# Down projections of a two-layer fp32 trunk: 16 of 22 row groups by Strassen's scheme, with DVE and ACT splitting the weights

## The chip, the core and the metric

The kernel runs on one core of one Trainium2 chip. The metric is the device time of one execution in microseconds, the median of several runs. All data are fp32. TensorE (PE) multiplies; VectorE (DVE), ScalarE (ACT) and GpSimd (POOL) work on data in SBUF, DVE and ACT also in PSUM; SyncE (SP) issues most DMAs.

## What is computed

Two residual layers on 512 tokens of 1024 channels. Each has a token mixer (forgetting attention, then an RG-LRU block), a layer norm, a gated ConvFFN, a second layer norm and a gated embedding. The change is in the ConvFFN's down projection, with D_FF = 2816:

```python
def conv_ffn(x, w_up, conv_w, conv_b, w_down):
    hdn = x @ w_up
    hdn = causal_dwconv(hdn, conv_w, conv_b)
    val, gate = jnp.split(hdn, [D_FF], axis=-1)
    return (jax.nn.gelu(gate) * val) @ w_down
...
        x = layer_norm(ALPHA * x + ff, ln2_g[i], ln2_b[i])
```

## The kernel before

**Precision.** Each fp32 operand is split into a high part (rounded to fp32r) and a low part (the difference). A product is three matmuls: high x high, high x low, low x high. `three` (L436) and `token_three` (L453) issue them, at L439 to L441 and L458 to L460.

**Weights.** They stream from HBM in units of 512 KB (128 partitions x 1024 elements) into four stages `stage`. SP loads a unit when POOL has split the one before it in that stage (`unit_split`, waits and loads up to L363). POOL then writes `w_hi` (L419) and, in four pieces, `w_lo` (L425) of one of four slots, as soon as PE has used the unit four places earlier (`unit_used`). `plan` (L120) lists the phases and slots in the order qkv, out0, up0, down0, ple0, gate0, rgx, rgg, out1, up1, down1, ple1, gate1, and every wait is a count in that order: `Phase.done(i, r)` is the count of a unit, `stage_free` and `slot_free` the counts at which its stage and slot are free. Each engine runs its own queue in program order.

**Up phase.** 11 iterations of four units (`up_phase`): a value and a gate tile for each of two halves, in PSUM banks 0 to 3, 24 matmuls a unit. For each half ACT applies the last tap of the convolution (L1436), DVE the two others (L1139, L1142), ACT the gelu (L1439), DVE the product (L1149); then ACT copies it to `h_hi` (L1442) and DVE subtracts to `h_lo` (L1154). DVE's and ACT's loops (both named `conv_ffn`, L1129 and L1425) are hardware loops over the 11 iterations. So `h` lies as 22 row groups of 128 channels by 512 tokens.

**Down phase** (`down_phase`, L794). The stationary operand is a 128 x 128 tile of `h` (channels x tokens), the moving one 512 output channels of a weight row. A unit holds two row groups for one half of the 1024 output channels, so there are 22 units a layer. For half 0 all four token tiles go through the 22 row groups side by side in four banks (4 x 22 x 3 matmuls). Half 1 does so for 16 row groups and finishes the last 6 token tile by token tile, with the transposes of the first normed tiles between (`turn_tile`).

**After it.** DVE adds `ALPHA * x` to each bank (`summed`, L969), normalises and writes `x` (L977, L982); `norm_low` (L987) writes `x_lo`. The embedding's input is loaded by ACT into the place of `x_hi` once the up phase is over (L1449).

What a wait on the weights looks like on PE, and on SP:

```python
            def unit_ready(ph, i, r):
                pe.wait_ge(unit_split, ph.done(i, r))
...
                        sp.wait_ge(unit_split, ph.stage_free(i, r))
```

## Time and profile before

| | |
|---|---|
| median of 3 runs | 1255.85 us (1255.59 to 1255.9) |
| profiled execution: span (the only time shown for it) | 1254.0 us |
| PE busy | 1246.9 us, 99% |
| PE weight loads | 1016.7 us, 81% |
| DVE busy | 551.0 us, 44% |
| ACT busy | 410.2 us, 33% |
| POOL busy | 861.5 us, 69% |
| DMA | 120.61 MB, 96 GB/s over the span |

The span runs from the first to the last instruction, so what lies around it is not in it. Busy times are of the profiled execution. Matmuls are pipelined: each is listed with its full length although the next starts before it ends, so what PE really spends on one is the distance of two starts. "x<-y" names what an instruction writes and reads; the bracket at the end of a timeline line is how long its engine had been idle and what ended that.

### The profile page before, as it was taken

What the parts mean: (1) busy time and instruction counts of PE and PEld (TensorE: products, weight loads), DVE (VectorE), ACT (ScalarE), POOL (GpSimd) and SP (SyncE); (2) the same over time, 40 slices, a digit from 0 to 9 for tenths busy, and PEclk for the clock granted to TensorE, in tenths of its full rate; (3) what the DMA queues carried; (4) which work ended last, traced back from release to release, by engine and by line L of the source; (5) the groups of instructions that cost most, each with busy time, mean ns of one, the idle gap of its engine ahead of it and who ended that gap; (6) DMA issues with size and microseconds to landing.
All of it is one profiled execution on the core that took longest, in us unless ns stands there. A gap on an engine that the chain in (4) does not pass through costs nothing.

```text
span 1254.0 us, 17715 instructions
## 1 busy us (share of the span) xinstructions
PE 1246.9 (99%) x5829; PEld 1016.7 (81%) x5829; DVE 551.0 (44%) x880; ACT 410.2 (33%) x684; POOL 861.5 (69%) x1154
## 2 busy tenths in 40 slices
PE   9999999999999999999999999999999999999998
PEld 6887777788888888888888778888888888888887
DVE  6556556564443444410444374364444443201352
ACT  4445444123434333100144484114343434100041
POOL 7555467629888777776577557929887787767573
PEclk9999999999999999999999999999999999999999
DMA  5221233303322233433143222312323224333221
GB/s 197 69 67 67 67 117 101 101 17 107 110 87 99 100 128 90 118 101 101 67 168 101 85 67 84 132 37 101 102 99 100 100 90 128 118 101 98 70 93 59
DMA packets 57292, 120.61 MB, mean 96 GB/s; under 512 B 3760, under 2 KB 36080, under 8 KB 56736
## 3 DMA queue, kind: packets, MB, share of 16 engines
q1 hardware_dynamic: 56192, 117.45, 28.8%
q10 hardware_dynamic: 1056, 2.58, 0.6%
q8 instruction: 26, 0.43, 0.1%
q14 instruction: 18, 0.15, 0.0%
HBM read 117.83 MB, written 2.20 MB: 96 GB/s over the span
## 4 chain that ended last, share of the span: by engine, by line
PE 97%; ACT 1%; DVE 1%; DMA 1%; issue 0%; DVEq 0%; ACTq 0%; SPq 0%
PE bank L439 19%; PE bank L440 19%; PE bank L441 19%; PE bank L458 9%; PE bank L459 8%; PE bank L460 8%; PE bank L735 2%; PE bank L740 2%; PE bank L733 2%; PE bank L554 1%; PE bank L541 1%; PE bank L467 1%; PE bank L525 1%; PE bank L523 1%; PE bank L909 1%; PE bank L910 1%
## 5 line engine op out<-in xcount | busy, mean ns | idle before, releaser
L425 POOL TENSOR_TENSOR w_lo<-stage,w_hi 128x256 fp32r<-128x256 f32 x800 | 593.8, 773 | 29.5 <-issue 1.5
L419 POOL TENSOR_SCALAR w_hi<-stage 128x1024 fp32r<-128x1024 f32 x200 | 213.8, 1069 | 172.8 <-PE bank L460 74.5
L439 PE MATMUL bank<-x_hi,w_hi 128*128 128x512 f32 (+1 forms) x712 | 275.7, 387 | 0.0
L441 PE MATMUL bank<-x_hi,w_lo 128*128 128x512 f32 (+1 forms) x712 | 275.3, 387 | 0.0
L440 PE MATMUL bank<-x_lo,w_hi 128*128 128x512 f32 (+1 forms) x712 | 275.3, 387 | 0.0
L439 PEld LDWEIGHTS bank<-x_hi,w_hi 128*128 128x128 f32 x712 | 133.7, 188 | 27.3
L441 PEld LDWEIGHTS bank<-x_hi,w_lo 128*128 128x128 f32 x712 | 133.7, 188 | 27.2
L440 PEld LDWEIGHTS bank<-x_lo,w_hi 128*128 128x128 f32 x712 | 133.7, 188 | 26.8
L1139 DVE SCALAR_TENSOR_TENSOR tmp<-bank,cols,tmp 128x511 f32<-128x511 f32 x88 | 66.0, 750 | 201.0 <-ACT tmp L1436 190.0
L458 PE MATMUL bank<-w_hi,h_hi 128*128 128x512 f32 x352 | 137.3, 390 | 0.0
L459 PE MATMUL bank<-w_lo,h_hi 128*128 128x512 f32 x352 | 137.0, 389 | 0.0
L460 PE MATMUL bank<-w_hi,h_lo 128*128 128x512 f32 x352 | 137.0, 389 | 0.0
L417 POOL TENSOR_TENSOR waiter<-waiter 128x1 f32<-128x1 f32 x101 | 21.2, 210 | 167.7 <-PE bank L441 112.2
L439 PE MATMUL bank<-in_hi,w_hi 128*128 128x512 f32 x312 | 130.0, 417 | 0.0
L441 PE MATMUL bank<-in_hi,w_lo 128*128 128x512 f32 x312 | 122.1, 391 | 0.0
L440 PE MATMUL bank<-in_lo,w_hi 128*128 128x512 f32 x312 | 122.0, 391 | 0.0
L969 DVE SCALAR_TENSOR_TENSOR bank<-x,bank 128x512 f32<-128x512 f32 x32 | 22.2, 693 | 191.3 <-PE bank L460 190.4
L1436 ACT ACTIVATE tmp<-bank,cols 128x512 f32<-128x512 f32 x88 | 63.8, 775 | 62.1 <-PE bank L441 60.8
L1294 ACT ACTIVATE norm_stat<-norm_stat 128x1 f32<-128x1 f32 x16 | 3.3, 206 | 227.6 <-DVE norm_stat L998 227.6
L460 PEld LDWEIGHTS bank<-w_hi,h_lo 128*128 128x128 f32 x352 | 66.1, 188 | 13.9
L458 PEld LDWEIGHTS bank<-w_hi,h_hi 128*128 128x128 f32 x352 | 66.1, 188 | 13.5
L459 PEld LDWEIGHTS bank<-w_lo,h_hi 128*128 128x128 f32 x352 | 66.1, 188 | 13.5
(180 smaller groups left out, 1804.6 us busy)
## 6 DMA issues: line engine op xcount, KB each, us to landing
stage<-w_square SPq DMA_DIRECT2D x163, 512.0 KB, 3.3
stage<-w_down SPq DMA_DIRECT2D x44, 512.0 KB, 3.7
rows<-norm_rows SPq DMA_DIRECT2D x4, 1024.0 KB, 5.7
outT<-x SPq DMA_DIRECT2D x7, 256.0 KB, 2.0
x<-xT SPq DMA_DIRECT2D x3, 512.0 KB, 6.8
p_in<-pT ACTq DMA_DIRECT2D x2, 512.0 KB, 3.2
w_ai<-w_lru SPq DMA_DIRECT2D x1, 1024.0 KB, 8.9
stage<-w_square ACTq DMA_DIRECT2D x1, 512.0 KB, 7.1
```

The source lines that it names most:

```text
L419: whole = pool.tensor_scalar(high[:, s, :], stage[:, s, :], 1.0, 0.0, ALU.mult, ALU.add)
L425: piece = pool.tensor_tensor(low[:, s, to], stage[:, s, to], high[:, s, to].bitcast(F32), ALU.subtract)
L439: pe.matmul(out, w_hi[:, s, c:c + P], m_hi, start=first, stop=False)
L440: pe.matmul(out, w_hi[:, s, c:c + P], m_lo, start=False, stop=False)
L441: return pe.matmul(out, w_lo[:, s, c:c + P], m_hi, start=False, stop=last)
L458: pe.matmul(four(out), m_hi, wide_hi, start=first, stop=False)
L459: pe.matmul(four(out), m_hi, wide_lo, start=False, stop=False)
L460: return pe.matmul(four(out), m_lo, wide_hi, start=False, stop=last)
L733: pe.matmul(at_banks[r][:, at], w_hi[:, s, c:c + P], x_hi[:, k, at], start=(k == 0), stop=False, skip_group_check=early > 0)
L735: pe.matmul(at_banks[r][:, at], w_lo[:, s, c:c + P], x_hi[:, k, at], start=False, stop=False, skip_group_check=early > 0)
L1139: dve.scalar_tensor_tensor(t[:, 1:SEQ], banks[r][:, 0:SEQ - 1], cols[:, bass.ds(c + 1, 1)], t[:, 1:SEQ], ALU.mult, ALU.add)
L1436: act.activation(tmp[:, r, :], banks[r][:], ACT.Identity, bias=cols[:, bass.ds(c + 3, 1)], scale=cols[:, bass.ds(c + 2, 1)]).then_inc(conv ...
```

## The change

The last 6 row groups of each layer's down projection stay as they were. The first 16 are taken in 8 pairs (`PRE`), one for each of the first 8 iterations of the up phase. For a pair, tokens, channels and output channels are each cut in two, and the 8 block products become 7 (Winograd's form), on sums of blocks.

- **Sums of h.** `gated_part` writes the product of the first 8 iterations unsplit into `folded`, and DVE's `fold_sides` forms four sums of 256 tokens. `h_hi` and `h_lo` remain for the last 6 row groups only.
- **Two loops on PE** (`fold_phase`). The first runs 3 products for each pair (18 matmuls, banks 6 and 7, 4 and 5, 0 and 1), the second 4 products (24 matmuls, adding in banks 4 to 7 and 0, 1, and in banks 2 and 3). Between the loops, and after the second, DVE adds banks into `x` (`block_fold`), and PE waits for it (`bank_folded`).
- **Units.** There are 32 fold units a layer instead of 16, each of the 16 loaded twice, in six stages: two more, `stage_far`, lie in the place of `x_hi` and `x_lo`, which the up phase reads to its end. So do two of the three pairs `side_hi`, `side_lo`.
- **Sums of weights.** In the first loop DVE adds the two blocks of the even unit (`first_sums`, 512 elements a partition). In the second POOL issues a DMA that adds one block of 256 KB from HBM onto the odd unit (`near_sum`), and DVE makes two sums from that (`second_sums`).
- **Splits.** ACT copies to the high part (`side_top`, `unit_top`), DVE subtracts to the low part (`side_low`, `unit_low`), for the sums of h as for the weights. POOL splits only the last six units of a down phase, after all of the fold units.
- **Order.** DVE's and ACT's up loops are written out instead of looped. The last half of the last iteration (convolution, gelu, product, split) is moved behind the end of the up phase, in between the steps 0 to 5 of the first loop.
- **Layer norm.** For the second norm `x` is already scaled and the bank is added plainly.

The diff, cut to its core:

```diff
+def fold_stage(r):
+    return [3, 0, 1, 2][r] if r < 4 else [3, 0, 4, 5, 1, 2][(r - 4) % FOLD_STAGES]
...
+            def down_loads(layer, ph):
+                for r in range(FOLD_UNITS):
+                    last = fold_before(r)
+                    if r < SLOTS:
+                        sp.wait_ge(unit_split, ph.stage_free(0, r))
+                    elif last is not None:
+                        sp.wait_ge(unit_split, ph.done(0, last))
+                    else:
+                        sp.wait_ge(unit_used, phases[f"up{layer}"].done(2 * FT // 4 - 1, 3))
+                    half = 1 - r % 2 if r < FOLD else r % 2
+                    sp.dma_start(staged(r).rearrange("p (a n) -> p a n", a=4),
+                                 down_unit(layer, half, r % FOLD // 2)).then_inc(fold_loaded[fold_stage(r)], 16)
...
+            def near_sum(layer, i):
+                r = FOLD + 2 * i + 1
+                pool.wait_ge(fold_loaded[fold_stage(r)], fold_fills(layer, r))
+                pool.dma_start(pair_of(staged(r))[:, :, 0, :], down_unit(layer, 0, i)[:, :, 0:P],
+                               accum_op=ALU.add).then_inc(near_summed[fold_stage(r)], 16)
...
+            def fold_product(layer, step, r, part, pos, bank, first, last):
...
+                for tau in range(2):
+                    to = slice(tau * P, (tau + 1) * P)
+                    m_hi, m_lo = side_hi[step % JIT][:, pos, to], side_lo[step % JIT][:, pos, to]
+                    out = four(banks[bank + tau])
+                    pe.matmul(out, m_hi, high, start=first, stop=False, skip_group_check=True)
+                    pe.matmul(out, m_hi, low, start=False, stop=False, skip_group_check=True)
+                    mm = pe.matmul(out, m_lo, high, start=False, stop=last, skip_group_check=True)
...
+                for i in range(PRE):
+                    first, last, step, r = i == 0, i == PRE - 1, PRE + i, FOLD + 2 * i
+                    unit_ready(ph, 0, r)
+                    pe.wait_ge(side_ready, layer * 2 * PRE + step + 1)
+                    if first:
+                        pe.wait_ge(bank_folded, layer * 6 + 2)
...
+            def second_sums(layer, i):
+                r = FOLD + 2 * i
+                dve.wait_ge(fold_loaded[fold_stage(r)], fold_fills(layer, r))
+                dve.wait_ge(near_summed[fold_stage(r + 1)], near_sums(layer, i))
+                far, near = pair_of(staged(r)), pair_of(staged(r + 1))
+                dve.tensor_tensor(far[:, :, 0, :], near[:, :, 0, :], near[:, :, 1, :], ALU.add)
+                dve.drain()
+                dve.tensor_tensor(far[:, :, 1, :], far[:, :, 0, :], far[:, :, 1, :], ALU.add)\
+                    .then_inc(fold_summed, 1)
...
+            def fold_down(layer):
+                ph, last = phases[f"down{layer}"], FT // 2 - 1
+                first_sums(layer, 0)
+                dve.wait_ge(unit_split, phases[f"up{layer}"].done(last, 3))
+                for i in range(PRE):
+                    side_low(layer, i)
+                    if i + 1 < PRE:
+                        first_sums(layer, i + 1)
+                    else:
+                        second_sums(layer, 0)
+                    unit_low(layer, 2 * i)
+                    unit_low(layer, 2 * i + 1)
+                    if i == 2:
+                        conv_part(layer, last, 1, 1)
+                    if i == 3:
+                        conv_part(layer, last, 1, 0)
+                    if i == 4:
+                        gated_part(layer, last, 1)
+                    if i == 5:
+                        h_low(layer, last, 1)
+                for i in range(PRE):
+                    r = FOLD + 2 * i
+                    side_low(layer, PRE + i)
+                    unit_low(layer, r)
+                    if i + 1 < PRE:
+                        second_sums(layer, i + 1)
+                    unit_low(layer, r + 1)
+                    if i == 0:
+                        dve.wait_ge(unit_used, ph.done(0, FOLD - 2))
+                        for tau in range(2):
+                            folded_in = block_fold(2 + tau, 1, 6 + tau, True, False)
+                        folded_in.then_inc(bank_folded, 1)
+                        dve.wait_ge(product_done, layer * 3 + 1)
+                        for tau in range(2):
+                            folded_in = block_fold(tau, 0, 4 + tau, True, True)
+                        folded_in.then_inc(bank_folded, 1)
...
+            def side_top(layer, step):
+                ph = phases[f"down{layer}"]
+                if step >= JIT:
+                    act.wait_ge(unit_used, ph.done(0, 2 * (step - JIT) + 1))
+                elif step:
+                    act.wait_ge(unit_used, phases[f"up{layer}"].done(FT // 2 - 1, 3))
+                act.wait_ge(fold_sides_ready, layer * PRE + step % PRE + 1)
+                act.copy(side_part(side_hi, step), side_of(step)).then_inc(side_high, 1)
```

## Rows read from the trace of the kernel before

**Rows 1.** The page's head: span and busy times.
```profile
span 1254.0 us, 17715 instructions
PE 1246.9 (99%) x5829; PEld 1016.7 (81%) x5829; DVE 551.0 (44%) x880; ACT 410.2 (33%) x684; POOL 861.5 (69%) x1154
```
**Rows 2.** The chain that ended last, share of the span by engine.
```profile
PE 97%; ACT 1%; DVE 1%; DMA 1%; issue 0%; DVEq 0%; ACTq 0%; SPq 0%
```
**Rows 3.** Timeline of PE at the start of down0 (start us, us, engine, line).
```profile
500.75 0.39 PE L458 MATMUL bank<-w_hi,h_hi 128*128 128x512 f32 x1
...
502.11 0.39 PE L458 MATMUL bank<-w_hi,h_hi 128*128 128x512 f32 x1
```
**Rows 4.** Busy time by stretch (length; PE, PEld, DVE, ACT, POOL; PEclk, DMA share, GB/s).
```profile
275.00:500.00 225.00, 225.00 (x995) 186.31 (x994) 100.75 (x126) 85.02 (x106) 185.73 (x254) 1.00 0.31 103
500.75:587.00 86.25, 86.25 (x382) 71.43 (x381) 19.20 (x34) 6.62 (x9) 63.03 (x80) 1.00 0.36 104
```
**Rows 5.** Timeline of POOL, one unit.
```profile
501.08 1.05 POOL L419 TENSOR_SCALAR w_hi<-stage 128x1024 fp32r<-128x1024 f32 x1 [0.73 <-PE bank L441]
502.27 2.84 POOL L425 TENSOR_TENSOR w_lo<-stage,w_hi 128x256 fp32r<-128x256 f32 x4
```
**Rows 6.** DVE: timeline around two places, then lines L1154 and L1080 by form.
```profile
502.17 0.75 DVE L1139 SCALAR_TENSOR_TENSOR tmp<-bank,cols,tmp 128x511 f32<-128x511 f32 x1 [3.11 <-ACT tmp L1436]
503.10 0.75 DVE L1142 SCALAR_TENSOR_TENSOR tmp<-bank,cols,tmp 128x510 f32<-128x510 f32 x1 [0.18 <-issue]
...
634.33 1.28 DVE L987 TENSOR_TENSOR x_lo<-bank,x_hi 128x512 fp32r<-128x512 f32 x2
636.58 0.69 DVE L987 TENSOR_TENSOR x_lo<-bank,x_hi 128x512 fp32r<-128x512 f32 x1 [0.97 <-ACT x_hi L1299]
...
L1154 DVE TENSOR_TENSOR h_lo<-tmp,h_hi x44: 691/904/1573, 283.3 to 1078.3; 128x512 f32 x44
...
L1080 DVE TENSOR_REDUCE stat<-bank 128x1 f32<-128x512 f32 x16 | 11.1, 691 | 1.2
...
L1080 DVE TENSOR_REDUCE stat<-bank 128x1 f32<-128x256 f32 x16 | 6.6, 412 | 0.0
```
**Rows 7.** ACT: timeline of the last iteration of up0, then line L1395 by form.
```profile
490.33 1.28 ACT L1436 ACT_TABLE_LOAD   x1 [4.67 <-PE bank L441]
...
501.24 1.45 ACT L1436 ACTIVATE tmp<-bank,cols 128x512 f32<-128x512 f32 x2 [3.27 <-PE bank L441]
...
511.53 1.14 ACT L1452 CAST p_hi<-p_in 128x512 fp32r<-128x512 f32 x2 [4.11 <-DMA p_in<-pT]
...
L1395 ACT COPY probs_t<-bank 128x384 f32<-128x384 f32 x32 | 15.5, 483 | 12.6 <-PE bank L541 12.6
...
L1395 ACT COPY probs_t<-bank 128x512 f32<-128x512 f32 x16 | 9.4, 588 | 6.3 <-PE bank L541 3.4 <-issue 2.6
```
**Rows 8.** DMA issues (KB each, us from issue to landing), and two issuing instructions.
```profile
stage<-w_down SPq DMA_DIRECT2D x44, 512.0 KB, 3.7
outT<-x SPq DMA_DIRECT2D x7, 256.0 KB, 2.0
w_ai<-w_lru SPq DMA_DIRECT2D x1, 1024.0 KB, 8.9
x<-xT ACTq DMA_DIRECT2D x1, 512.0 KB, 9.0
...
2.22 1.00 ACTq L1313 DMA_DIRECT2D bf<-b_forget  x1
...
L363 SPq DMA_DIRECT2D stage<-w_down x16: 367/368/372, 500.4 to 581.3; - x16
```
**Rows 9.** Busy time by stretch, the best half microsecond of one w_down load.
```profile
540.00:540.50 0.50, 0.50 (x4) 0.42 (x3) 0.00 (x0) 0.00 (x0) 0.35 (x2) 1.00 1.07 379
```
**Rows 10.** The same view at the end of the span, after the last matmul (1250.4).
```profile
1253.00:1253.50 0.50, 0.00 (x0) 0.00 (x0) 0.00 (x0) 0.00 (x0) 0.00 (x0) 1.00 0.28 92
1253.50:1254.00 0.50, 0.00 (x0) 0.00 (x0) 0.00 (x0) 0.00 (x0) 0.00 (x0) 0.57 0.00 0
```

More of the change, by code:

```diff
@@ L133, in plan @@
     for name, slots, iters in want:
+        own = FOLD_UNITS if name.startswith("down") else 0
         last_used[SLOTS:] = [first - 1] * SLOTS
@@ L319, in rounds, with staged, pair_of, fold_fills @@
                     yield i
+        def staged(r):
+            s = fold_stage(r)
+            return stage[:, s, :] if s < SLOTS else stage_far[:, s - SLOTS, :]
+        def pair_of(unit):
+            return unit.rearrange("p (a b n) -> p a b n", a=4, b=2)
+        def fold_fills(layer, r):
+            s = fold_stage(r)
+            each = [fold_stage(n) for n in range(FOLD_UNITS)]
+            return 16 * (layer * each.count(s) + each[:r + 1].count(s))
+        def near_sums(layer, i):
+            near = [fold_stage(FOLD + 2 * n + 1) for n in range(PRE)]
+            return 16 * (layer * near.count(near[i]) + near[:i + 1].count(near[i]))
+        def down_unit(layer, half, kp):
+            u = layer * KT + half * 4
+            return w_down[u:u + 4, :, kp * 2 * P:(kp + 1) * 2 * P].rearrange("a p n -> p a n")
+        def side_of(step):
+            return folded[:, step % PRE, 0:3, :] if step < PRE else folded[:, step % PRE, 3:7, :]
+        def side_part(tile, step):
+            return tile[step % JIT][:, 0:3 if step < PRE else 4, :]
         def one(t, m):
@@ L343, in _ @@
                 base, n, layer = square_first, len(ph.slots), int(name[-1]) if name[-1] in "01" else 0
+                if name.startswith("down"):
+                    down_loads(layer, ph)
+                    continue
                 for i in rounds(sp, ph):
@@ L373, in _ @@
                     square_first += 2 * n
-                elif name != "rgx" and not name.startswith("down"):
+                elif name != "rgx":
                     square_first += ph.iters * n
@@ L796, in down_phase @@
                 ph = phases[f"down{layer}"]
[L797 to L809 removed]
+                fold_phase(layer)
@@ L1211, in rest_of_layer @@
                 conv_ffn(layer)
+                fold_down(layer)
                 embed(layer)
```

335 lines of the change are left out of this document (257 added, 78 removed).

## The prediction

> **What bounds the kernel now.** I read the page's head first [rows 1]: PE is busy 1246.9 of the 1254.0 us span, while DVE (44%) and ACT (33%) have room. The chain that ended last [rows 2] is 97% PE. So a removed matmul is time won, as long as nothing else comes late. The reader should then see what one matmul costs: it is listed at 0.39 us, but the timeline [rows 3] starts six from 500.75 to 502.11, so one costs 1.36 / 6 = 0.2267 us, and the first down projection starts at 500.75 right behind the last up matmul. From there to 587 PE has no gap, at a granted clock of 1.00 [rows 4]. The 44% of DVE is an average; what counts here is the stretch of the down projections, where DVE has been nearly empty (19.2 of 86.25 us) and is now given POOL's work.
>
> The profiled execution spans 1254.0 us; no other time is shown for it, and the median of the three runs lies 1.85 us above. I sum changes against the span and add them to 1255.85. About 0.2%, 2.5 us, is what a measurement of this kernel can tell from no change.
>
> **PE's share.** The 16 row groups took 4 token tiles x 16 x 2 halves x 3 = 384 matmuls a layer. Now 8 pairs take 7 products of 6 matmuls, 336. 48 x 0.2267 = 10.9 us a layer, **21.8 us** in all, if PE never waits. A step of the first loop (18 matmuls) lasts 4.08 us, one of the second (24) 5.44 us, both loops 76.2 us.
>
> **What one DVE and ACT instruction costs.** Before, POOL split the weights in 1.05 + 2.84 us for each unit of 5.44 us [rows 5]. DVE and ACT now do it, in fold_down and unit_top. A DVE pair on 512 elements is listed at 0.69 us, but two in a row took 1.28 [rows 6], so a second costs 0.60. The reductions of 512 and 256 elements, 0.691 and 0.412, give 1.09 ns an element; so 768 elements cost 0.87 and 1024 cost 1.15; a drain between dependent ones adds 0.2 to 0.3 (two instructions of 0.75 start 0.93 apart at 502.17, where the overlap of 0.09 would leave 0.66, [rows 6]; I take 0.22). h_lo took up to 1.57 us while POOL worked beside it and 0.69 at best [rows 6]; POOL only issues DMAs in the two loops, so I take the uncontended value. An ACT copy of two tiles took 1.14 [rows 7]: 0.52 each in a row, and with 0.82 ns an element (0.588 and 0.483 for 512 and 384) 0.73 and 0.94 for 768 and 1024; it stays under 3.3 us a step and is not the bound. PE to ACT takes 0.49 (500.75 to 501.24), ACT to DVE 0.15.
>
> DVE's step in the first loop is side_low 0.87, first_sums 0.60, unit_low 0.60 + 1.15 = 3.22 of 4.08 us. In the second it is 3 x 1.15 and second_sums 1.42 (two of 0.60 and a drain), 4.87 of 5.44 us. So it fits on average, without much room, and the convolution of the last half, the PSUM folds and the waits come on top.
>
> **The layer in order of time,** t = 0 at the first fold matmul. Before it nothing is late: the last h_lo of the first half ends near -3.3 (half 0 began 10.9 us earlier; unrolled, its two table loads of 1.28 us ([rows 7] shows the first) should go, since the other half of the old loop body ran without them), which leaves DVE time for units 0 and 1. Then:
> - side_high for step 1 lies where x_hi was, so ACT may write it only after the last up matmul, and behind the two convolution activations (1.45 us for both, [rows 7]). DVE gets it at 0.49 + 1.35 + 0.73 + 0.15, about 2.75. Steps 1 to 6 take 6 x 3.22 = 19.3, the held-back convolution of the last half adds 4 x 0.80 = 3.2, its product and h_lo 1.2, side_low(7) 0.87: DVE reaches second_sums(0) at 27.3. PE wants unit 14, behind it in DVE's order, at 28.6.
> - second_sums(0) also waits for the accumulating DMA on unit 17. SP loads that unit only when unit_low(11) has freed its stage, at 2.75 + 5 x 3.22 + 3.2 + 0.6 = 22.65; landing takes 3.7 [rows 8] and about 0.6 behind unit 16, so 26.95. Then POOL issues the accumulation, which takes A. DVE waits until 26.95 + A.
> - From there second_sums 1.42, unit_low(14) and (15) 1.75, side_low(8) and unit_low(16) 2.30, second_sums(1) 1.42, unit_low(17) 1.15, four folds out of PSUM 2.40, hand-over 0.2: 10.6 us until bank_folded is 2, for which the second loop's first matmul waits. Ideal is 32.6. PE is late by 26.95 + A + 10.65 - 32.6 = **5.0 + A**. All of this is one queue: behind the wait in second_sums stand the low halves of units that are long there.
> - In the second loop the same chain closes on itself: unit_low(17) frees a stage, load 23 (4.3 with its issue), A, second_sums(3) 1.42, unit_low(21) 1.15, and so three times until unit 29. PE wants that unit 6.5 steps, 35.4, after the loop's start, which lies 2.6 behind unit_low(17), hand-over 0.2 off: the excess is 3 x (6.87 + A) - 37.8 = **3A - 17.2**, when positive.
> - At the end six folds (3.6) fit between product_done and the rest units but for 0.2.
>
> Both layers: 2 x (5.0 + A + 0.2 - 10.9 + max(0, 3A - 17.2)) = 2 x (A - 5.7 + max(0, 3A - 17.2)). **All turns on A.** No accumulation, and no DMA from POOL, is in the trace. It moves 256 KB in and has to read the 256 KB that lie there. Lower bound: a 256 KB transfer landed in 2.0 us; upper: 9.0 for a 512 KB one beside others [rows 8]. A load of 512 KB, the same bytes, took 3.7; at the 379 GB/s of the best half microsecond [rows 9] one unit already in flight puts 1.4 before it (two units a step now ask for 190 to 260 GB/s, where the old down stretch had 104, [rows 4]); and making 512 row pieces on POOL costs at least the 1.00 us of the longest ACT issue [rows 8]. A = 3.7 + 1.4 + 1.0 = 6.1, nearest to the 3.7 row. That gives 2 x (0.4 + 1.1) = 3.0 us: **1258.9 us**. Ends: A = 2.0 gives -7.4 (1248), A = 9.0 gives +26 (1282).
>
> By the Trainium skill, DMA: Bandwidth & Descriptors, section Anatomy of one DMA, a POOL DMA costs about 2.0 us plus bytes / 436 GB/s; that is an estimate of 2.6 us here, and the sum would be 6 us below before, 1250. No run shows it yet.
>
> **Other edits.** In the up phase each of the first 8 iterations loses two h_lo and gains four 256-element sums with drains, about 2.2 us against 1.4, and DVE is busy 100.75 of 225 us there [rows 4]; ACT loses two copies. Nothing. If that cover were gone it would be 8 x 0.8 a layer. The layer norm's first instruction changes its form and not its 0.69 us. The weights are loaded twice (16 more units of 512 KB a layer), SP's issues of 0.37 us [rows 8] fit twice into a step. The folded PSUM adds replace nothing and are counted above. The last 6 row groups keep their POOL splits, which start 5 us before their use.
>
> **Rivals.**
> 1. The accumulation is quick, A up to 4.4. For it: the 2.0 us transfer. Then DVE's queue holds PE back by less than was saved (with no wait for the DMA at all it is 27.3 + 10.65 + 0.2 - 32.6 = 5.5 a layer): A = 3 gives -5.4, **1250**. Chance 0.26. The Trainium skill's page on DMA, named above, stands on this side.
> 2. DVE is not the limit: the loops run at PE's pace and most of 21.8 stays, 1234 to 1245. For it: averages of 3.22 against 4.08; against: the 10.6 us queue at the turn of the loops, which holds for A = 0 too. 0.05.
> 3. A between 4.4 and 6.0: the gain and the waits cancel, **1256**. 0.25.
> 4. Slow accumulation: from A = 5.73 each further microsecond costs 8 us in all. A = 8 gives 2 x (2.3 + 6.8) = +18, **1274**. For it: w_ai took 8.9 us. 0.15 of the 0.44 that I give to slower; the other 0.29 is the forecast's own case.
> 5. PE's clock. PE now idles over 4 us at unit 14 and again before the second loop. At the end of the span the clock was still 1.00 until 3.1 us after the last matmul and 0.57 in the next half microsecond [rows 10]. Half speed in step 7 is hidden by the folds; 12 slow matmuls at the second loop's start cost up to 2.7 us a layer, 5.4, **1264**, less where the accumulation binds anyway. Part of slower. The Trainium skill, TensorE: Matmul & The Clock Gate, section HAM oscillation, says that waits for DMA between matmul groups can drop the array to half rate and each group restarts cold.
> 6. ACT keeps its table loads: two of 1.28 near t = 0 push DVE's chain by up to 2.6 us a layer, 1264. Small.
>
> **How the numbers follow.** Forecast 0.29, with rivals 4 to 6 slower in all 0.44; same 0.25; faster 0.31. The range reaches from A = 2 with DVE a little shorter an instruction (1246) to A = 8.1 (1275); the ends beyond hold 2 in 10.
>
> **What would show it.** Matmul groups of the fold count 2 x 56 x 6 = 672 over both layers, at 0.2267 apart inside a step. PE's waits: about 1 us at unit 2, 1 in steps 3 and 4, 4 to 6 at unit 14, 4 to 4.5 before the second loop, one or more in its second half, near nothing at the rest units. DVE's longest wait is second_sums on the DMA, 5 to 6 us once a layer and then every second step. Wrong if the accumulation lands in under 4 us, if DVE intervals are not 0.60 and 1.15, if PE stalls in other places, or if the table loads stand.

## The result, and the profile after

The changed kernel takes **1271.34 us** (median of four runs, 1268.15 to 1273.62) against 1255.77 (1255.59 to 1255.90) for the kernel before in the same comparison: ratio 1.0122, 95% interval 1.0111 to 1.0134. That is 15.6 us slower where the prediction had 3.0. The direction was right and the time is inside the range of 1246 to 1275, but four fifths of the loss were not foreseen. The profiled execution took 1271.83 us, 1.7 us more than its span, as before.

The page's head and the chain that ended last, to be held against [rows 1] and [rows 2]:

```profile
span 1270.1 us, 17075 instructions
PE 1236.9 (97%) x5733; PEld 1003.4 (79%) x5733; DVE 711.8 (56%) x1096; ACT 422.2 (33%) x706; POOL 743.5 (59%) x1010
...
PE 83%; DVE 7%; DMA 7%; ACT 1%; issue 1%; DVEq 1%; ACTq 0%
```

PE has 96 matmuls less, as announced (48 a layer), but is busy only 10.0 us less instead of 21.8, and the chain, 97% PE before, now runs through DVE and DMA for 7% each. (PE's busy time fell by less than 21.8 us mostly because some 9 us of it are matmuls at half clock, shown below.) So the saving was made and more than spent. Where, the same table of stretches as [rows 4] shows for layer 0 (length; PE, PEld, DVE, ACT, POOL with instruction counts; granted clock, DMA share, GB/s):

```profile
505.00:530.00 25.00, 24.77 (x108) 20.11 (x108) 22.19 (x29) 15.84 (x21) 1.47 (x1) 1.00 0.85 268
530.00:550.00 20.00, 11.93 (x39) 8.98 (x38) 15.42 (x20) 6.22 (x7) 3.80 (x3) 0.83 0.75 154
550.00:586.00 36.00, 33.58 (x141) 27.27 (x140) 27.62 (x29) 16.75 (x17) 5.06 (x4) 0.95 0.75 175
536.00:537.00 1.00, 1.00 (x3) 0.81 (x4) 1.00 (x2) 1.00 (x2) 0.00 (x0) 0.50 0.27 23
```

Almost all of the first loop runs at PE's pace; the 20 us around the turn of the two loops lose 8 us of PE. The last row says something else: while PE is at work again in 536 to 537, the granted clock is 0.50, the lower of its two levels (1.2 GHz). The timelines of PE, DVE and POOL around that place (start, duration, engine, line; in brackets the idle time before and what ended it):

```profile
505.18 0.50 PE L894 MATMUL bank<-w_hi,side_hi 128*128 128x512 f32 x1 [0.38 <-DVE w_lo L1375]
...
535.73 0.80 PE L894 MATMUL bank<-w_hi,side_hi 128*128 128x512 f32 x1 [5.39 <-DVE w_lo L1375]
536.33 0.63 PE L895 MATMUL bank<-w_lo,side_hi 128*128 128x512 f32 x1
536.75 0.63 PE L896 MATMUL bank<-w_hi,side_lo 128*128 128x512 f32 x1
...
544.12 0.47 PE L894 MATMUL bank<-w_hi,side_hi 128*128 128x512 f32 x1 [2.68 <-DVE x L1382]
...
578.38 0.50 PE L894 MATMUL bank<-w_hi,side_hi 128*128 128x512 f32 x1 [2.42 <-DVE w_lo L1375]
...
1124.04 0.47 PE L894 MATMUL bank<-w_hi,side_hi 128*128 128x512 f32 x1 [2.53 <-DVE x L1382]
```
```profile
526.38 0.95 DVE L1363 TENSOR_TENSOR side_lo<-folded,side_hi 128x768 fp32r<-128x768 f32 x1
533.62 0.69 DVE L1355 TENSOR_TENSOR stage<-stage 128x512 f32<-128x512 f32 x1 [6.28 <-DMA stage<-w_down]
...
548.27 0.69 DVE L1355 TENSOR_TENSOR stage<-stage 128x512 f32<-128x512 f32 x1 [0.65 <-DMA stage<-w_down]
...
561.69 0.69 DVE L1355 TENSOR_TENSOR stage_far<-stage_far 128x512 f32<-128x512 f32 x1 [3.54 <-DMA stage_far<-w_down]
...
575.73 0.69 DVE L1355 TENSOR_TENSOR stage<-stage 128x512 f32<-128x512 f32 x1 [3.93 <-DMA stage<-w_down]
```
```profile
527.90 1.47 POOL L496 DMA_DIRECT2D stage<-w_down  x1 [44.47 <-DMA stage<-w_down]
...
541.81 1.26 POOL L496 DMA_DIRECT2D stage<-w_down  x1 [9.01 <-DMA stage<-w_down]
...
554.83 1.25 POOL L496 DMA_DIRECT2D stage_far<-w_down  x1 [6.30 <-DMA stage_far<-w_down]
```

Read them together. DVE is done with side_low(7) at 527.3 and would go on, but second_sums(0) (L1355) waits 6.28 us for the accumulating DMA, which POOL could issue only at 527.90, when unit 17 had landed. The low halves of units 14 and 15 stand behind that wait, so PE stands still for 5.39 us at unit 14 and again for 2.68 us at the turn. In the second loop DVE waits at every second step, and the sums are 13.4 and 14.0 us apart there (548.27, 561.69, 575.73), where two steps of PE are 10.9. PE waits for this at unit 27 (578.38). The row at 1124.04 is the turn in layer 1.

I counted, over the matmul starts of each layer's down phase and norm, what lies beyond the 0.2267 us of [rows 3]:

| where | layer 0 | layer 1 |
|---|---|---|
| gap at unit 2 (and slow matmuls at unit 6) | 0.53 + 0.32 | 0.53 + 0.31 |
| gap at unit 14, half clock behind it | 5.54 + 1.43 | 6.61 + 1.54 |
| gap at the turn of the loops, half clock | 2.83 + 1.65 | 2.69 |
| gaps in the second loop, half clock | 2.58 + 1.67 | 1.24 + 3.72 + 1.68 |
| gap ahead of the layer norm's turned tiles | 2.05 | 0 |

Together, with small ones, some 38 us more than before; less the 21.8 saved this is about 16, and the spans differ by 16.1. "Half clock" is what the matmuls that start 0.427 us apart take beyond 0.2267.

The DMA issues (KB each, us from issue to landing), for [rows 8], and the software queue (packets, MB):

```profile
stage<-w_down SPq DMA_DIRECT2D x56, 512.0 KB, 4.6
stage_far<-w_down SPq DMA_DIRECT2D x20, 512.0 KB, 4.7
...
stage<-w_down POOLq DMA_DIRECT2D x10, 256.0 KB, 5.8
...
stage_far<-w_down POOLq DMA_DIRECT2D x6, 256.0 KB, 4.9
```
```profile
q0 software_dynamic: 8448, 4.20, 2.7%
```

A plain load, 3.7 us before, lands in 4.6 now. The doubled number of loads is not all of that: in e1_no_sum below, which has as many loads but no DMA from GpSimd, those into `stage` land in 3.8 (those into `stage_far` in 4.6). The accumulation of half as many bytes takes longer than a load.

The last row of the table above has a cause of its own. DVE's timeline behind layer 0's folds:

```profile
600.55 1.02 DVE L1454 TENSOR_SCALAR lam<-cols 128x8 f32<-128x8 f32 x1
...
604.62 4.92 DVE L1105 SCALAR_TENSOR_TENSOR lam<-lam 128x8 f32<-128x8 f32 x7
...
611.74 0.69 DVE L1120 TENSOR_TENSOR bank<-bank,x 128x512 f32<-128x512 f32 x1
```

decay_rates, 11.2 us of tiny instructions, used to lie in DVE's idle time beside the down projection. In program order it stands behind it, and DVE is now busy there to the end, so the norm's first sum starts only at 611.74.

### The profile page after: what moved, and what is told of

The parts are those of the page before. It is cut to its first block, busy times and chain, and to the rows that moved or that the text cites. A ratio compares the mean times of both kernels' runs of the same rounds, so it can differ in the third digit from the quotient of the medians.

```text
span 1270.1 us, 17075 instructions
## 1 busy us (share of the span) xinstructions
PE 1236.9 (97%) x5733; PEld 1003.4 (79%) x5733; DVE 711.8 (56%) x1096; ACT 422.2 (33%) x706; POOL 743.5 (59%) x1010
## 3 DMA queue, kind: packets, MB, share of 16 engines
q0 software_dynamic: 8448, 4.20, 2.7%
q10 hardware_dynamic: 1056, 2.58, 0.6%
## 4 chain that ended last, share of the span: by engine, by line
PE 83%; DVE 7%; DMA 7%; ACT 1%; issue 1%; DVEq 1%; ACTq 0%
PE bank L538 19%; PE bank L540 19%; PE bank L539 19%; DMA stage<-w_down 5%; PE bank L557 3%; PE bank L559 3%; PE bank L558 3%; PE bank L832 2%; PE bank L839 2%; PE bank L834 2%; DVE w_lo L1375 2%; DMA stage_far<-w_down 2%; PE bank L653 1%; PE bank L640 1%; PE bank L566 1%
## 5 line engine op out<-in xcount | busy, mean ns | idle before, releaser
L524 POOL TENSOR_TENSOR w_lo<-stage,w_hi 128x256 fp32r<-128x256 f32 x672 | 484.7, 754 | 26.5 <-issue 3.6
L518 POOL TENSOR_SCALAR w_hi<-stage 128x1024 fp32r<-128x1024 f32 x168 | 183.3, 1091 | 133.7 <-PE bank L540 53.7
L539 PEld LDWEIGHTS bank<-x_lo,w_hi 128*128 128x128 f32 x712 | 133.7, 188 | 27.3
L538 PEld LDWEIGHTS bank<-x_hi,w_hi 128*128 128x128 f32 x712 | 133.7, 188 | 26.8
L894 PE MATMUL bank<-w_hi,side_hi 128*128 128x512 f32 x224 | 91.8, 410 | 25.0 <-DVE w_lo L1375 19.7
L496 POOL DMA_DIRECT2D stage<-w_down x10 | 12.9, 1288 | 138.4 <-DMA stage<-w_down 138.4
L896 PE MATMUL bank<-w_hi,side_lo 128*128 128x512 f32 x224 | 90.2, 403 | 0.0
L895 PE MATMUL bank<-w_lo,side_hi 128*128 128x512 f32 x224 | 90.0, 402 | 0.0
L894 PEld LDWEIGHTS bank<-w_hi,side_hi 128*128 128x128 f32 x224 | 43.9, 196 | 38.6 <-DVE w_lo L1375 23.6
L1289 DVE SCALAR_TENSOR_TENSOR tmp<-bank,cols,tmp 128x510 f32<-128x510 f32 x88 | 65.9, 748 | 7.4 <-issue 0.9
L540 PEld LDWEIGHTS bank<-in_hi,w_lo 128*128 128x128 f32 x312 | 58.6, 188 | 13.0
L538 PEld LDWEIGHTS bank<-in_hi,w_hi 128*128 128x128 f32 x312 | 58.7, 188 | 12.7 <-issue 3.1
```

The lines of the kernel that those rows point to most:

```text
L518: whole = pool.tensor_scalar(high[:, s, :], stage[:, s, :], 1.0, 0.0, ALU.mult, ALU.add)
L524: piece = pool.tensor_tensor(low[:, s, to], stage[:, s, to], high[:, s, to].bitcast(F32), ALU.subtract)
L538: pe.matmul(out, w_hi[:, s, c:c + P], m_hi, start=first, stop=False)
L539: pe.matmul(out, w_hi[:, s, c:c + P], m_lo, start=False, stop=False)
L540: return pe.matmul(out, w_lo[:, s, c:c + P], m_hi, start=False, stop=last)
L894: pe.matmul(out, m_hi, high, start=first, stop=False, skip_group_check=True)
```

## The experiments

Theory A: the wait for the accumulation inside second_sums, with DVE's queue behind it. Rivals: the doubled plain loads (B), too much work for DVE (C), the hop to another engine (D), the half clock as a cost of its own (E).

**Without the accumulation (e1_no_sum).**
```diff
-                    for i in range(PRE):
-                        near_sum(int(name[-1]), i)
...
-                dve.wait_ge(near_summed[fold_stage(r + 1)], near_sums(layer, i))
+                dve.wait_ge(fold_loaded[fold_stage(r + 1)], fold_fills(layer, r + 1))
```


> The eight accumulating DMAs of a layer are left out, so one of the eight left-matrix sums of the second loop lacks a block (that part of the computation is missing); second_sums waits for the plain load of the near unit instead; all instructions on DVE, ACT and PE stay. Theory A (the wait for the accumulation inside second_sums, with DVE's 10.6 us of work queued behind it, makes the PE gaps at unit 14, at the turn of the loops and at unit 27): the gap at unit 14 falls from 5.5 to 6.6 us to under 2 us, those of the second loop to about 0; with the half clock after them gone too, 1271.3 falls by 20 to 24 us to 1247 to 1251. Rival B (the plain loads, twice as many bytes in the same time, set the pace): the gaps stay within 2 us of what they were, since only 1 MB of about 9 MB a layer is gone: 1265 to 1270. Rival C (DVE has too much work in these loops): nothing is taken from DVE, so 1270 or more.

Measured: 1251.34 us, ratio to before 0.9963 (0.9949 to 0.9978). 20 us came off with the wait and 2.1 MB of traffic a layer (the 1 MB of the expectation was too little). The gaps at unit 14 and in the second loop are gone; besides 0.4 us at unit 2 and 2.0 at the norm, what PE still waits for in layer 0 is

```profile
538.30 0.47 PE L891 MATMUL bank<-w_hi,side_hi 128*128 128x512 f32 x1 [3.81 <-DVE x L1379]
```

Theory A in the main. C is out, since DVE's work was the same, and so is B: there were as many loads. They did land somewhat sooner (`stage` 3.8 us instead of 4.6), so this run alone does not part the wait from the traffic; e5_plain_dma below keeps the traffic. But the turn is not free without the accumulation either: 4.0 us of gap in each layer, and 1.7 and 2.4 us of half clock behind it.

**The same sum on DVE (e2_dve_sum), and on GpSimd (e3_pool_sum).**
```diff
-                dve.wait_ge(near_summed[fold_stage(r + 1)], near_sums(layer, i))
+                dve.wait_ge(fold_loaded[fold_stage(r + 1)], fold_fills(layer, r + 1))
                 far, near = pair_of(staged(r)), pair_of(staged(r + 1))
+                dve.tensor_tensor(near[:, :, 0, :], near[:, :, 0, :], far[:, :, 0, :], ALU.add)
+                dve.drain()
```


> The same sum as the accumulating DMA makes is made by one more tensor_tensor of 512 columns on DVE at the head of second_sums, from the copy of the block that the far unit's load has brought (0.60 us and a drain, 0.22 to 0.7 us), eight times a layer; no accumulating DMA. Theory A: as without the sum, less 8 x 0.9 us a layer of which the cycle of 5.44 us against DVE's 4.87 hides about half: 1249 to 1254. Rival B (loads): 1265 to 1272. Rival C (DVE overloaded): slower than the changed kernel, 1275 to 1285.


```diff
-                pool.wait_ge(fold_loaded[fold_stage(r)], fold_fills(layer, r))
-                pool.dma_start(pair_of(staged(r))[:, :, 0, :], down_unit(layer, 0, i)[:, :, 0:P],
-                               accum_op=ALU.add).then_inc(near_summed[fold_stage(r)], 16)
+                for n in (r - 1, r):
+                    pool.wait_ge(fold_loaded[fold_stage(n)], fold_fills(layer, n))
+                far, near = pair_of(staged(r - 1)), pair_of(staged(r))
+                pool.tensor_tensor(near[:, :, 0, :], near[:, :, 0, :], far[:, :, 0, :], ALU.add)\
+                    .then_inc(near_summed[fold_stage(r)], 1)
```


> The same sum is made by one tensor_tensor of 512 columns on the idle GpSimd (estimate 1.5 to 2 us, from its 2.84 us for a subtraction of 1024 columns), after the loads of the far and the near unit; no accumulating DMA. Theory A: A falls from 6 us to about 2 us, under the 4.4 us from which on the forecast has it decide: 1247 to 1253. Rival D (what costs is that the sum lies on another engine at all, one semaphore hop more in the chain, or that GpSimd and DVE at work together slow each other): 1260 or more, and DVE's instructions beside it longer than 0.60 and 1.13 us. Rival B: 1265 to 1270.

Measured: on DVE 1254.28 us (0.9991, 0.9981 to 1.0000), on GpSimd 1257.99 (1.0019, 1.0010 to 1.0029). The block is in SBUF already, brought by the far unit's load; adding it there with 0.77 us of DVE takes 17 us off the kernel. Rival C is out for good: DVE has more to do and the kernel is faster. On GpSimd the sum is as early but not as cheap. The groups of DVE in 500 to 585 (busy us, mean ns), on GpSimd's kernel and then on DVE's:

```profile
L1377 DVE TENSOR_TENSOR w_lo<-stage,w_hi 128x1024 fp32r<-128x1024 f32 x15 | 20.5, 1368 | 0.0
L1365 DVE TENSOR_TENSOR side_lo<-folded,side_hi 128x1024 fp32r<-128x1024 f32 x8 | 13.0, 1629 | 0.0
```
```profile
L1374 DVE TENSOR_TENSOR w_lo<-stage,w_hi 128x1024 fp32r<-128x1024 f32 x15 | 18.3, 1220 | 0.0
L1362 DVE TENSOR_TENSOR side_lo<-folded,side_hi 128x1024 fp32r<-128x1024 f32 x8 | 9.8, 1219 | 0.0
```

On average the same instructions take 12% and 34% longer here, beside GpSimd's sums of 1.29 to 2.29 us, and the timeline shows where. A low half of 1024 elements that DVE starts while one of the sums is under way takes 2.30 to 2.36 us (ten in both layers, as at 532.07 and 542.86), all others 1.22; a low half already under way when the sum starts keeps its 1.22, and the sum takes longer (2.13 us at 541.95, 2.16 at 551.43). So the part of rival D about the two engines slowing each other is right. The Trainium skill, SBUF — State Buffer, section Who interferes with whom, says that a DVE instruction with two SBUF inputs contends with a GpSimd instruction that reads SBUF; the trace agrees.

**Filler matmuls in the gaps (e4_warm, e7_dve_warm).**
```diff
+            def keep_busy(layer, n):
+
+                pe.wait_ge(tile_read[f"up{layer}"], 2 * FT)
+                pe.wait_ge(h_lo_ready, layer * FT + 2 + FOLD + 1)
+                for _ in range(n):
+                    pe.matmul(banks[2][:], h_hi[:, 0, 0:P], h_hi[:, 0, :], start=True, stop=True)
...
+                    if last:
+                        keep_busy(layer, 22)
                     unit_ready(ph, 0, 2 * i)
...
                     if first:
+                        keep_busy(layer, 8)
                         pe.wait_ge(bank_folded, layer * 6 + 2)
```


> 22 matmuls whose result nobody reads are put on PE before unit 14 and 8 before the wait for the folded banks at the turn of the loops, each 0.227 us and together 5.0 and 1.8 us, less than the gaps there (5.5 to 6.6 and 2.7 to 2.8 us), so that they delay nothing and only keep PE at work. Theory E (the half clock after these gaps costs time of its own): the matmul interval of 0.427 us right after them is gone, and with it 1.4 + 1.7 us in layer 0 and 1.5 us in layer 1: 1265.5 to 1268. Rival F (DVE sets the pace there, so PE's slow matmuls only fill what would be a wait): the interval is 0.227 us but the gaps behind grow by the same, 1270.5 to 1272.

Measured: 1272.36 us (1.0139, 1.0122 to 1.0156), no faster than the changed kernel. Stretches of this kernel:

```profile
536.00:537.00 1.00, 1.00 (x5) 0.82 (x6) 1.00 (x2) 1.00 (x2) 0.00 (x0) 1.00 0.08 12
545.00:546.00 1.00, 1.00 (x6) 0.78 (x6) 1.00 (x2) 0.00 (x0) 0.00 (x0) 1.00 0.66 119
567.00:569.00 2.00, 2.00 (x6) 1.60 (x5) 1.84 (x3) 1.14 (x2) 0.00 (x0) 0.50 0.87 144
```

The clock is 1.00 where it was 0.50, and nothing is won: in layer 0 a gap of 2.9 us with half clock behind it opened in the second loop instead (the last row is just behind it). Rival F: the slow matmuls at unit 14 and at the turn of the changed kernel fill time in which PE would wait for DVE and the accumulation. Those behind the last gap of the changed kernel's second loop (1.7 us in each layer) it did not cover, and no later wait hides them: the one at layer 0's norm stands behind DVE's last folds, which themselves wait for PE (589.86, 3.36 us). I put the same filler, 18 matmuls, before the turn of the kernel with the sum on DVE, where nothing comes late behind the turn:

> e2_dve_sum (1254.3) with 18 matmuls whose result nobody reads (4.08 us) in PE's gap of 4.9 us at the turn of the loops. In e2_dve_sum no gap follows in the second loop, so here PE sets the pace behind the turn. Theory E2 (half clock costs where PE sets the pace): the matmul interval behind the turn is 0.227 instead of 0.427 us, 2.5 and 2.1 us come off: 1249.3 to 1250.5. Rival F2 (DVE, with 5.77 us of work a step against PE's 5.44, is just behind and takes it back in the second loop): 1253 to 1254.5, with gaps of 0.3 us a step instead.

Measured: 1252.43 us (0.9968, 0.9955 to 0.9982), 1.9 us less than without the filler. By the median neither expectation, between the two. The same stretch without and with the filler:

```profile
541.00:543.00 2.00, 2.00 (x6) 1.61 (x5) 2.00 (x3) 0.00 (x0) 0.00 (x0) 0.50 0.00 0
```
```profile
541.00:543.00 2.00, 2.00 (x10) 1.65 (x9) 2.00 (x4) 0.00 (x0) 0.00 (x0) 1.00 0.04 13
```

In the profiled executions the mechanism is theory E2's: from its first matmul to its last, the second loop ran 2.8 and 2.3 us over PE's pace in e2_dve_sum, which is the half clock, and 0.1 in both layers here. DVE, with 5.55 us a step in the timeline (its side_low starts at 558.30, 563.85 and 569.40) against PE's 5.44, did not take it back. So half clock cost its full 4.9 us where PE sets the pace. The time fell by less because other things came later: in layer 1 DVE waited 1.43 us for a plain load ahead of unit 14, and the first fold matmul already stood 0.9 us later, before any filler runs.

**A plain DMA in the place of the accumulating one (e5_plain_dma).**
```diff
                 pool.dma_start(pair_of(staged(r))[:, :, 0, :], down_unit(layer, 0, i)[:, :, 0:P],
-                               accum_op=ALU.add).then_inc(near_summed[fold_stage(r)], 16)
+                               ).then_inc(near_summed[fold_stage(r)], 16)
```


> The DMA on GpSimd's queue stays, with its 512 packets and its wait, but overwrites the near block instead of adding to it (the near block is missing from the sums: that part of the computation is left out). Theory A1 (the addition on the way makes the transfer long): it lands 3 to 3.7 us after its issue instead of 4.7 to 5.8, and the time falls to 1260 to 1265. Theory A2 (issue on GpSimd, one small transfer behind the full queues of the loads, and the landing make it up, added or not): landing as before within 0.5 us, 1269 to 1272.

Measured: 1258.37 us (1.0024, 1.0013 to 1.0035). 13 us hang on the word accumulate. Its software queue, its issues and two of its waits:

```profile
q0 software_dynamic: 1280, 4.20, 1.1%
...
stage<-w_down POOLq DMA_DIRECT2D x10, 256.0 KB, 4.3
...
stage_far<-w_down POOLq DMA_DIRECT2D x6, 256.0 KB, 3.2
```
```profile
527.81 0.96 POOL L496 DMA_DIRECT2D stage<-w_down  x1 [44.27 <-DMA stage<-w_down]
...
553.08 0.75 POOL L496 DMA_DIRECT2D stage_far<-w_down  x1 [5.74 <-DMA stage_far<-w_down]
```
```profile
532.12 0.69 DVE L1354 TENSOR_TENSOR stage<-stage 128x512 f32<-128x512 f32 x1 [4.66 <-DMA stage<-w_down]
...
558.66 0.69 DVE L1354 TENSOR_TENSOR stage_far<-stage_far 128x512 f32<-128x512 f32 x1 [2.97 <-DMA stage_far<-w_down]
```

The same 4.20 MB go in 1280 packets instead of 8448, that is 80 of 3.3 KB a transfer against 528 of about 0.5 KB, POOL needs 0.75 us to issue one instead of 1.26, and it lands 1.5 to 1.7 us sooner. From POOL's start to DVE's, the A of the prediction, it is 4.31 and 5.58 us against 5.72 and 6.86. So 1.3 to 1.4 us less of A gave 13.0 us, 10 for one. The plain loads landed in 4.5 us, nearly as before (4.6), so it is not their landing.

**Which of the eight accumulations costs (e9_first_dve, e10_only_first).** The first sum on DVE and seven by DMA:
```diff
+                if i:
                     dve.wait_ge(near_summed[fold_stage(r + 1)], near_sums(layer, i))
+                else:
+                    dve.wait_ge(fold_loaded[fold_stage(r + 1)], fold_fills(layer, r + 1))
...
+                if i == 0:
+                    dve.tensor_tensor(near[:, :, 0, :], near[:, :, 0, :], far[:, :, 0, :], ALU.add)
+                    dve.drain()
```


> The changed kernel with the first of the eight sums of a layer (that of unit 17, waited for ahead of unit 14) made on DVE as in e2_dve_sum, the other seven by accumulating DMAs. Theory A' (each of the two places is enough by itself: DVE comes to the second sum 5 us earlier, finds that accumulation not landed either, and the chain load, accumulation, sums, low half of 13.4 to 14 us against two steps of 10.9 us sets the pace from there): the gap at unit 14 goes from 5.5 to about 1 us, that at the turn grows from 2.8 to about 8, and the time stays at 1269 to 1273. Rival I (the places add up): only the 5.5 us and the half clock behind it go, in both layers: 1257 to 1261.

and the opposite (the two conditions exchanged):

> The opposite: the first sum of each layer by the accumulating DMA, the other seven on DVE. Theory A': the gap at unit 14 stays at 5 to 6 us and that at the turn at 4 to 5, there are none in the second loop: 1260 to 1265, so that the seven later accumulations cost 6 to 11 us beside the first. Rival I (places add up): e2_dve_sum's 1254.3 and 2 x 6 us and the half clock behind them, 1267 to 1269.

Measured: 1270.45 us (1.0107, 1.0091 to 1.0122) and 1263.40 (1.0060, 1.0044 to 1.0076). PE's waits in layer 0, of the one and of the other:

```profile
543.87 0.77 PE L894 MATMUL bank<-w_hi,side_hi 128*128 128x512 f32 x1 [8.78 <-DVE x L1388]
```
```profile
535.81 0.79 PE L893 MATMUL bank<-w_hi,side_hi 128*128 128x512 f32 x1 [5.43 <-DVE w_lo L1380]
544.96 0.47 PE L893 MATMUL bank<-w_hi,side_hi 128*128 128x512 f32 x1 [3.02 <-DVE x L1387]
```

Both times are as theory A' has them; only the gap at the turn with the first sum by DMA (3.02 us, 2.4 in layer 1) is shorter than its 4 to 5. Taking the first wait away alone gives 0.9 us, which is less than the runs of one kernel differ: DVE runs into the second accumulation, and PE's gap moves from unit 14 to the turn and grows to 8.78 us. Taking the seven others away gives 7.9 us, all eight 17.1. The costs do not add up; they are one chain.

**The rest of layer 0's path (e6_lam), the order at the turn (e8_turn), GpSimd's start (e11_early), and all three beside the DMA (e12_repairs_dma).** decay_rates and its Exp before the up projection:
```diff
+                if layer == 0:
+                    decay_rates()
                 conv_ffn(layer)
                 fold_down(layer)
                 embed(layer)
-                if layer == 0:
-                    decay_rates()
```


> Of the changed kernel only decay_rates (DVE, about 8 us) and its Exp on ACT are moved: from behind the down projection of layer 0 to before the up projection. Theory G (this work, which lay in DVE's idle time of the down phase before the change, now stands before layer 0's norm): PE's gap of 2.05 us at the norm of layer 0 falls to about 0 and the time to 1269.0 to 1269.8. Rival H (the norm waits for other things, the fold of the last banks and its drains): 1271 to 1272.

Measured: 1269.50 us (1.0099, 1.0084 to 1.0115). PE has no gap at layer 0's norm any more, so theory G is right about the cause of that gap. The 1.8 us less can't be put down to it: the runs of the two kernels overlap (1266.37 to 1269.84 and 1268.15 to 1273.62), and in the profiled executions layer 0, from its first fold gap to the norm, took 129.0 us against 128.4, while layer 1, where nothing was moved, took 125.0 against 128.2. Then the sum on DVE, this, and the folds of banks 6 and 4 ahead of second_sums(1):
```diff
                     unit_low(layer, r)
+                    if i == 0:
+                        dve.wait_ge(unit_used, ph.done(0, FOLD - 2))
...
+                        folded_in.then_inc(bank_folded, 1)
                     if i + 1 < PRE:
                         second_sums(layer, i + 1)
                     unit_low(layer, r + 1)
                     if i == 0:
-                        dve.wait_ge(unit_used, ph.done(0, FOLD - 2))
...
-                        folded_in.then_inc(bank_folded, 1)
                         dve.drain()
```


> e2_dve_sum with decay_rates moved as in e6_lam, and at the turn of the loops the four folds that PE waits for put before second_sums(1) and the low half of unit 17 instead of behind them. Theory A (the gap at the turn is DVE's queue of 10.6 us, of which 2.9 us stand ahead of the folds without need): the gap falls from 4.9 to about 1.7 us, followed by three of 0.6 to 0.9; no half clock, and the gap at the norm gone: 1254.3 - 1.2 - 5 - 2 = 1246, 1245 to 1248. Rival F2 (DVE's total work from the turn on decides, in whatever order): 1251 to 1252, the 2 us of the norm alone.

Measured: 1249.05 us (0.9944, 0.9930 to 0.9958), 5.2 less than e2_dve_sum. In the profiled executions 4.0 us of it come between the first fold matmuls of the two layers and 1.3 behind; the edit of decay_rates is in layer 0 only, so about 2 us fit the gap at the norm. PE's waits in layer 0:

```profile
537.01 0.47 PE L891 MATMUL bank<-w_hi,side_hi 128*128 128x512 f32 x1 [1.51 <-DVE x L1381]
540.19 0.50 PE L891 MATMUL bank<-w_hi,side_hi 128*128 128x512 f32 x1 [0.20 <-DVE w_lo L1374]
543.84 0.50 PE L891 MATMUL bank<-w_hi,side_hi 128*128 128x512 f32 x1 [0.62 <-DVE w_lo L1374]
547.12 0.50 PE L891 MATMUL bank<-w_hi,side_hi 128*128 128x512 f32 x1 [0.26 <-DVE w_lo L1374]
```

The one gap of 4.7 us became four, in all 2.6 us (0.63 more stand at unit 14); no half clock follows (mean granted clock 1.000), and the median is 1 us above the expected interval. A gap of 1.05 us a layer was left at the rest units, where GpSimd starts only when DVE has written unit 31:
```diff
-                        if ph.own and r == ph.own:
-                            pool.wait_ge(unit_split, ph.done(0, r - 1))
...
                             to = slice(c, c + UNIT // PIECES)
+                            if ph.own and r == ph.own and c == UNIT - UNIT // PIECES:
+                                pool.wait_ge(unit_split, ph.done(0, r - 1))
```


> e8_turn (1249.05), and GpSimd may begin with the first rest unit before DVE has written the low half of unit 31: its wait for that stands before its last piece instead of before the unit. In e8_turn it writes eight units back to back from there, 4.0 us each, and PE waits 1.05 us for one of them in each layer. Theory J (that wait is all of it): both gaps go and the time is 1246.9 to 1247.5. Rival K (GpSimd's work now lies beside DVE's, which it slows: e3_pool_sum's low halves took 1.37 us beside it, not 1.22): 1248.5 to 1250.

Measured: **1247.34 us** (0.9933, 0.9919 to 0.9946). GpSimd's first copy there starts at 575.79 instead of 578.26, and takes longer beside DVE:

```profile
575.79 1.88 POOL L513 TENSOR_SCALAR w_hi<-stage 128x1024 fp32r<-128x1024 f32 x1 [92.14 <-DMA stage<-w_down]
577.82 3.63 POOL L521 TENSOR_TENSOR w_lo<-stage,w_hi 128x256 fp32r<-128x256 f32 x4
```

Both gaps all but go (0.48 and none), 1.7 of 2.1 us. This version is faster than both kernels: 0.7% under before, 24 us under the change. Last, the same three repairs on the kernel with its accumulating DMA:

> The three repairs of e11_early (decay_rates early, folds ahead of second_sums(1) at the turn, GpSimd's wait late) on the changed kernel with its accumulating DMA kept. Theory A' (the chain load, accumulation, two sums, low half decides, so that putting the folds ahead only lets PE wait for the next accumulation instead; second_sums(1) even comes 2.7 us later and with it the load behind it): of e6_lam's 1269.5 the order takes nothing off: 1268 to 1272. Rival L (the queue at the turn is the loss, with or without the accumulation): as from e2_dve_sum to e11_early, 5 us less than e6_lam: 1263 to 1266.

Measured: 1265.88 us (1.0082, 1.0066 to 1.0099), 3.6 us less than e6_lam and 5.5 less than the changed kernel, between the expectations. PE's waits in layer 0 from the turn on:

```profile
541.85 0.47 PE L894 MATMUL bank<-w_hi,side_hi 128*128 128x512 f32 x1 [0.19 <-DVE x L1382]
547.91 0.50 PE L894 MATMUL bank<-w_hi,side_hi 128*128 128x512 f32 x1 [0.33 <-DVE w_lo L1375]
558.26 0.50 PE L894 MATMUL bank<-w_hi,side_hi 128*128 128x512 f32 x1 [1.91 <-DVE w_lo L1375]
571.67 0.50 PE L894 MATMUL bank<-w_hi,side_hi 128*128 128x512 f32 x1 [0.63 <-DVE w_lo L1375]
```

The gap at the turn is all but gone, and waits in the second loop remain. The table sets the profiled executions side by side. Late at the turn: how much later than 144 x 0.2267 us after the first fold matmul the second loop starts. Inside: how much longer than PE's pace it takes from its first matmul to its last.

| | layer 0: at the turn, inside | layer 1: at the turn, inside |
|---|---|---|
| changed kernel | 10.9, 6.1 | 12.0, 6.9 |
| e1_no_sum | 5.0, 1.7 | 5.0, 2.5 |
| e2_dve_sum | 6.4, 2.8 | 6.1, 2.3 |
| e3_pool_sum | 7.3, 2.7 | 7.2, 3.0 |
| e7_dve_warm | 6.3, 0.1 | 7.5, 0.1 |
| e8_turn | 3.6, 2.6 | 3.3, 2.6 |
| e4_warm | 10.8, 6.7 | 10.6, 6.8 |
| e5_plain_dma | 9.3, 1.0 | 9.4, 0.1 |
| e9_first_dve | 10.4, 4.1 | 11.5, 8.3 |
| e10_only_first | 11.7, 1.7 | 11.0, 0.1 |
| e6_lam | 10.7, 9.1 | 10.7, 4.0 |
| e12_repairs_dma | 8.4, 6.1 | 8.9, 6.9 |

Against e6_lam, the repairs took 2.3 and 1.8 us off at the turn, and inside the second loops the sum is the same (13.1 us in both, 13.0 in the changed kernel). So against theory A' the order did take something off with the accumulation kept, though less than the 2.8 us a layer that it gave from e2_dve_sum to e8_turn. How much of it is order and how much is when transfers happened to land (accumulations into `stage` landed in 5.2 us here, 5.8 in the changed kernel) stays open; the runs of one kernel with accumulation spread over 2.6 to 5.5 us, those of before over 0.3 to 1.1.

## Why the prediction came out as it did

- **PE's share and the instruction prices held.** 96 matmuls less; DVE's intervals inside runs are 0.60, 0.87 and 1.13 us (0.60, 0.87, 1.15 forecast). DVE reached second_sums(0) 26.8 us after the first fold matmul (forecast 27.3), the table loads went, the up phase cost nothing.
- **The wait was where it was put:** DVE's longest in layer 0's first loop is second_sums on the DMA, 6.28 us, then every second step, and PE stood still at unit 14 and at the turn. The term 5.0 + A, the lateness at the start of the second loop (11.1 with A = 6.1), measured 10.9 us in layer 0 and 12.0 in layer 1. A, from POOL's start to DVE's, was 5.7 and 6.8 us there. Of the gap forecast ahead of the loop, 4 to 4.5 us, 2.7 to 2.8 came, with 1.4 to 1.5 us of half clock behind unit 14 in the place of the rest.
- **The step that failed is the term of the second loop, "3 x (6.87 + A) - 37.8".** It was mis-sized: forecast 1.1 us a layer; measured inside the loop 6.1 and 6.9. Of that, 4.3 and 5.2 are PE behind the chain (the half clock at layer 0's turn is hidden in it), and 1.7 in each layer is half clock behind the last gap, for which the sum had nothing. Why the chain was longer:
  - The prediction followed it over the odd sums (unit_low(17), load 23, second_sums(3), and so on to unit 29). The one that binds runs over the even sums: unit_low(15), load 21, second_sums(2), 4 and 6, and PE is late at unit 27. At the prediction's own prices that is 3A - 16.6, 1.7 us instead of 1.1.
  - The load, with its issue, took 5.1, 4.0 and 5.1 us in layer 0 and 5.1, 4.9 and 6.9 in layer 1 (4.3 forecast, from the 3.7 of [rows 8] at half the traffic): 1.3 and 4.1 us more. This is the largest part.
  - A was 6.5, 6.9 and 6.4 us in layer 0, 6.0, 6.6 and 5.3 in layer 1 (6.1 forecast): 1.4 us more and 0.4 less.
- **Inside the range partly by luck.** The upper end of the range stood for A = 8.1. A was close to its forecast, 5.3 to 6.9, and the time came near that end by the load and the half clock instead. Nor is the slope of the formula confirmed: 8 us for one of A holds only above 5.73, and from 6.1 to 4.8 the formula gives 4.8 us, where the plain DMA, 1.3 to 1.4 us quicker, took 13.0 off. In the profiled executions 11.9 us of that are inside the second loops, with their half clock.
- **A term that was missing: layer 0's norm, 2.05 us.** The prediction costed the embedding and decay_rates at nothing by not naming them. Their cover was DVE's idle time during the down projection (19.2 us busy of 86.25, [rows 4]), and the change filled it. Moving them took the gap away (e6_lam).
- The rest units, "0.2", cost nothing in the changed kernel, and 1.05 us a layer in e8_turn, once PE came there early.
- Added up over both layers: 10.8 for the second loop, 2.05 for the norm, 0.7 for the turn, less 0.4 for the rest units make 13.1, as the spans have it (16.1 against 3.0).
- **Rival 5, the clock,** was right that the granted clock falls to 0.50, but the idle time alone does not say when: it fell behind 5.39, 2.68 and 2.42 us of idle time in layer 0, and stayed at 1.00 behind 2.53 at the turn of layer 1 and behind 1.51 in e8_turn. Of its price, the part at unit 14 and at the turn gave nothing when it was removed (e4_warm); what lies behind the last gap, 1.7 us a layer, has no later wait to hide in, and where no accumulation binds the filler took the full 4.9 us out of the second loops (1.9 by the medians). The Trainium skill, TensorE: Matmul & The Clock Gate, section HAM oscillation, says that waits between matmul groups drop the array to half rate: the trace agrees (the 0.50 in 536 to 537).
- **Rival 1, a quick accumulation,** fell with its figure. By the Trainium skill, DMA: Bandwidth & Descriptors, section Anatomy of one DMA, it would take an estimated 2.6 us; it took 4.9 and 5.8 from issue to landing, and without accumulating 3.2 and 4.3. The measurement decides. With no wait for a DMA the forecast gave 5.5 us a layer of lateness, so 1245; measured 1251.3, and the 2.1 us of the norm and 4.1 of half clock behind the turn are as much as the difference.

## What to carry to other kernels

A wait put into the middle of an in-order queue costs what stands behind it, and when the same buffers come round again it closes a loop: each link's error is multiplied, here 1.3 us of each transfer into 13. Work out the chain for every buffer of the ring, not for one of them. Price it with durations under the traffic that the change itself makes, and try first whether the data is in SBUF already: 0.77 us of the "loaded" engine beat 6 us of a free one. When an engine's idle time is filled, list everything that used to hide in it, to the end of the phase.

## What the runs showed that I had not expected

- An accumulating DMA of 256 KB went in 528 packets of about 0.5 KB, the plain one of the same shape in 80; 0.5 us more of issue on GpSimd and 1.5 to 1.7 us more to land.
- 512-element sums on GpSimd took 1.29 to 2.29 us, and a low half of 1024 elements that DVE started beside one took 2.30 to 2.36 us instead of 1.22.
- GpSimd's 16 small DMAs made the loads beside them land later: 4.6 us with them (4.5 when they do not accumulate), 3.8 without, for the same loads into `stage`.
- Keeping PE's clock up was worth nothing where PE was waiting anyway, although the trace shows the matmuls at 0.43 us an interval turn back into 0.23. Where PE set the pace it was worth all that the slow matmuls add up to.
